# Moving a 128x128 transpose of attention weights from TensorE to a DMA, in a fused decoder layer

## The reference

```python
h = h + 0.5 * swiglu(rms_norm(h, ffn1_norm), ffn1_w_in, ffn1_w_out)     # hidden width 2816
n = rms_norm(h, mix_norm)
gm_u, gm_v, sb_q, sb_k, sb_v = split(n @ w_mix_in)                      # 512 channels each
gm_out = gelu(gm_u) * (tril(w_s) @ rms_norm(gelu(gm_v)) + b_s)          # in chunks of 128 tokens
# stick-breaking attention, 8 heads of 64, for t > s:
#   z[t,s] = q[t].k[s] / 8
#   A[t,s] = sigmoid(z[t,s]) * prod over s<j<t of (1 - sigmoid(z[t,j]))
sb_out = A @ v
h = h + concat(gm_out, sb_out) @ w_mix_out
h = h + 0.5 * swiglu(rms_norm(h, ffn2_norm), ffn2_w_in, ffn2_w_out)
h = h + sigmoid(rms_norm(h, ple_norm) @ ple_w_gate) * (p @ ple_w_proj)
out = rms_norm(h, final_norm)
```

## Time and profile before

| what | value |
|---|---|
| median of 3 runs | 4325.1 us (4325.03 to 4327.18) |
| the profiled execution's own time | 4324.56 us |
| its span, first to last instruction, slowest core (core 3) | 4323.0 us |
| spans of the 8 cores | 4313.9 to 4323.0 us |
| mean granted TensorE clock, core 3 | 0.903 |
| instructions | 66727 |

### The profile page before, as it was taken

How to read it: one execution, slowest core, us unless ns; L and a number is a source line. 1 busy time by engine, 2 the same in 40 slices (tenths; PEclk the granted TensorE clock), 3 DMA queues, 4 the chain that set the end, 5 groups by cost and what they waited for, 6 DMA issues and landing times.

```text
span 4323.0 us, 66727 instructions; the slowest of 8 cores (4313.9 to 4323.0 us)
## 1 busy us (share of the span) xinstructions
PE 3549.6 (82%) x18821; PEld 1641.0 (38%) x18821; DVE 2812.3 (65%) x3660; ACT 1835.6 (42%) x2945; POOL 1082.2 (25%) x654
## 2 busy tenths in 40 slices
PE   6689787979797988979697997988879877777687
PEld 2234332434343433434243443433434333333233
DVE  3244646355655666567776787867878778887743
ACT  2232434143424444444444454554445445444522
POOL 1111222011212222223232332332323333444300
PEclk9889897989898999989898997988989988898789
DMA  8964694524342334323332333322324221111043
GB/s 278 320 206 124 211 319 148 146 82 127 104 140 83 116 92 141 111 81 111 101 112 83 91 113 88 104 83 72 86 76 118 78 62 43 39 44 43 26 120 102
DMA packets 254387, 499.66 MB, mean 116 GB/s; under 512 B 28074, under 2 KB 47058, under 8 KB 254034
## 3 DMA queue, kind: packets, MB, share of 16 engines
q1 hardware_dynamic: 251858, 493.29, 38.0%
q0 software_dynamic: 2176, 2.10, 0.4%
HBM read 436.03 MB, written 61.34 MB: 115 GB/s over the span
## 4 chain that ended last, share of the span: by engine, by line
PE 53%; DVE 18%; issue 12%; ACT 8%; DMA 3%; SPq 3%; POOL 3%; DVEq 1%; ACTq 0%; POOLq 0%
PE bank L169 49%; DVE P L202 8%; PE bank L172 4%; SPq L208 3%; POOL A L191 3%; ACT bank L182 2%; DVE P L185 2%; DVE xnT L199 2%; ACT AT L182 2%; DVE ef_62 L191 1%; DMA fstv_95<-wts 1%; DVE ef_63 L191 1%; ACT L182 1%; ACT rr L182 1%; DVE hT_56 L199 1%
## 5 line engine op out<-in xcount | busy, mean ns | idle before, releaser
L202 DVE TENSOR_TENSOR_SCAN P<-bank,P,cb 128x512 f32<-128x512 f32 (+3 forms) x1152 | 1375.8, 1194 | 509.0 <-ACT bank L182 414.8
L191 POOL TENSOR_TENSOR A<-P 128x1024 bf16<-128x1024 f32 (+3 forms) x576 | 1008.9, 1752 | 2739.4 <-DVE P L202 1578.1
L182 ACT ACTIVATE AT<-bank 128x1024 bf16<-128x1024 bf16 (+3 forms) x576 | 546.6, 949 | 689.2 <-PE bank L172 688.2
L182 ACT ACTIVATE bank<-bank 128x512 f32<-128x512 f32 (+3 forms) x1152 | 579.7, 541 | 204.5 <-PE bank L169 194.2
L172 PE MATMUL bank<-cb,A 128*128 128x128 bf16 x4224 | 363.8, 233 | 206.9 <-POOL A L191 153.9
L172 PEld LDWEIGHTS bank<-cb,A 128*128 128x128 bf16 x4224 | 295.6, 104 | 382.2 <-issue 317.4
L169 PE MATMUL bank<-AT,vc 128*128 128x256 bf16 x2112 | 360.9, 294 | 34.7 <-DVE mix_59 L185 18.5
L185 DVE COPY P<-P 128x2 f32<-128x2 f32 x448 | 269.2, 601 | 15.9 <-DVE P L202 14.5
L169 PEld LDWEIGHTS bank<-AT,vc 128*128 128x128 bf16 x2112 | 200.8, 103 | 203.5 <-issue 109.7
L182 ACT ACTIVATE ef_62<-bank 128x512 f32<-128x512 f32 x240 | 142.9, 595 | 305.9 <-PE bank L169 287.2
L182 ACT ACTIVATE ef_63<-bank 128x512 f32<-128x512 f32 x240 | 142.7, 594 | 228.8 <-PE bank L169 217.4
(11 more groups left out here) (237 smaller groups left out, 4643.4 us busy)
## 6 DMA issues: line engine op xcount, KB each, us to landing
ring_73<-wscr SPq DMA_DIRECT2D x102, 256.0 KB, 2.7
ring_76<-wscr SPq DMA_DIRECT2D x101, 256.0 KB, 2.6
ring_67<-wscr SPq DMA_DIRECT2D x101, 256.0 KB, 2.6
ring_70<-wscr SPq DMA_DIRECT2D x101, 256.0 KB, 2.7
ring_71<-wscr SPq DMA_DIRECT2D x100, 256.0 KB, 2.7
ring_74<-wscr SPq DMA_DIRECT2D x100, 256.0 KB, 2.7
ring_77<-wscr SPq DMA_DIRECT2D x100, 256.0 KB, 2.6
ring_68<-wscr SPq DMA_DIRECT2D x99, 256.0 KB, 2.7
```

Source lines behind the costliest of these rows:

```text
L182: return lambda e: e.activation(out, in_, func, **kw)
L191: return lambda e: e.tensor_tensor(out, in0, in1, op)
L202: return lambda e: e.tensor_tensor_scan(out, d0, d1, initial, op0, op1)
```

## The change

The transposes leave PE and ACT: one DMA per step, issued by SP, transposes the whole 128x1024 `A` buffer into `AT` as eight 128x128 blocks. `A` is zeroed once, since the DMA reads all of it in diagonal steps too. `AT` gets four buffers, and `stage_v` runs five steps after `stage_a` (LAG) where it ran three after. The carry column moves from DVE to POOL, with its own dependency (`Pc`), and the scan takes its start from the buffer of the step before. The copies out of bank 4 move from DVE to ACT and go to a single buffer `sbT`; a new gate `O` holds the first of them until the mix-out projection of the tile before is emitted. Bank 3 goes to the side stream. In ple, the product is written back to PSUM, not to the SBUF buffer `ef`. The costs handed to the scheduler are new, and an engine no longer waits in the model for its own results.

```diff
+SA = 2
+ST = 4
+LAG = 5
-MM_NS = 1.0 / 2.2
+MM_NS = 0.475
...
+def f_dmat(out, in_):
+    return lambda e: e.dma_start_transpose(out=out, in_=in_)
...
-        side = BankPool([5, 6, 7])
-        wide = BankPool([0, 1, 2, 4, 5, 6, 7])
+        side = BankPool([3, 5, 6, 7])
+        wide = BankPool([0, 1, 2, 3, 4, 5, 6, 7])
...
-                S.op("dve", f_tt(efb[i][:, :], efb[i][:, :], B(bj), ALU.mult), reads=[ef_res[i], bank_res[bj]], writes=[ef_res[i]], cost=dve_cost(T))
-                S.op("dve", f_tt(hT[:, j, :], hT[:, j, :], efb[i][:, :], ALU.add), reads=[ef_res[i]] + hr(j), writes=hr(j), cost=dve_cost(T))
+                S.op("dve", f_tt(B(bj), efb[i][:, :], B(bj), ALU.mult), reads=[ef_res[i], bank_res[bj]], writes=[bank_res[bj]], cost=dve_cost(T))
+                S.op("dve", f_tt(hT[:, j, :], hT[:, j, :], B(bj), ALU.add), reads=[bank_res[bj]] + hr(j), writes=hr(j), cost=dve_cost(T))
...
-                if kc == ti:
-                    S.op("dve", f_memset(Pb[:, s, :, c0:c0 + 1], 1.0), writes=[P_res[s]], cost=90.0)
-                else:
-                    S.op("dve", f_copy(Pb[:, s, :, 0:1], Pb[:, 1 - s, :, T:T + 1]), reads=[P_res[1 - s]], writes=[P_res[s]], cost=90.0)
...
-                S.op("pool", f_tt(Ab[:, s, :, c0:T], Pb[:, s, :, c0:T], Pb[:, s, :, c0 + 1:T + 1], ALU.subtract), reads=[P_res[s]], writes=[A_res[s]], cost=2 * n_ * 2.2 + 120)
+                    init = 1.0 if kc == ti else Pb[:, 1 - s, h, T:T + 1]
...
+                if kc == ti:
+                    S.op("pool", f_memset(Pb[:, s, :, c0:c0 + 1], 1.0), writes=[Pc_res[s]], cost=150.0)
+                else:
+                    S.op("pool", f_copy(Pb[:, s, :, 0:1], Pb[:, 1 - s, :, T:T + 1]), reads=[P_res[1 - s]], writes=[Pc_res[s]], cost=150.0)
+                sa = n % SA
+                S.op("pool", f_tt(Ab[:, sa, :, c0:T], Pb[:, s, :, c0:T], Pb[:, s, :, c0 + 1:T + 1], ALU.subtract), reads=[P_res[s], Pc_res[s]], writes=[A_res[sa]], cost=2 * n_ * 1.65 + 205)
...
             def stage_t(n):
-                s = n % 2
-                k0 = c_lo(n) // 128
-                for kb in range(k0, 4):
-                    for h in range(2):
-                        o0 = (kb * 2 + h) * 128
-                        S.op("pe", f_tr(banks[3][:, o0:o0 + 128], Ab[:, s, h, kb * 128:(kb + 1) * 128], identb), reads=[A_res[s], R_const], writes=[bank_res[3]], cost=60.0)
-                act(ATb[:, s, k0:4, :].rearrange("p a b -> p (a b)"), banks[3][:, k0 * 256:1024], AF.Copy, [bank_res[3]], [AT_res[s]])
+                s = n % ST
+                sa = n % SA
+                S.op("sp", f_dmat(ATb[:, s, :, :], Ab[:, sa, :, :].rearrange("p h t -> p (h t)")), reads=[A_res[sa]], writes=[AT_res[s]], dma="t%d" % s, cost=1300.0)
...
-                        S.op("dve", f_copy(mixb[ti % 2][r, 4 + hp, qb * 128:(qb + 1) * 128], B(4)[r, h * 128:(h + 1) * 128]),
-                             reads=[bank_res[4]], writes=[mix_resb[ti % 2][4 + hp]], cost=dve_cost(128))
+                        act(sbT[r, hp, qb * 128:(qb + 1) * 128], B(4)[r, h * 128:(h + 1) * 128], AF.Copy, [bank_res[4]], [sb_res[hp]])
...
-            for n in range(N + 3):
-                if 0 <= n - 2 < N:
-                    yield [A_res[n % 2], bank_res[3]]
-                    stage_t(n - 2)
+            for n in range(N + LAG):
...
+                m = n - LAG
+                if 0 <= m < N:
+                    ti = items[m][0]
+                    if items[m][3] == 0 and ti > 0 and items[m][1:3] == (0, 0):
+                        yield ("gate", ("O", ti - 1))
+                    yield [AT_res[m % ST], bank_res[4]]
+                    stage_v(m)
+                if 0 <= n - 1 < N:
+                    stage_t(n - 1)
```

More of the change, by code:

```diff
@@ L43, in __init__, with ready @@
         self.dma_clk = 0.0
-    def ready(self, reads, writes):
+    def ready(self, reads, writes, eng):
         t = 0.0
         for r in reads:
-            if r.wt > t:
+            if r.we != eng and r.wt > t:
                 t = r.wt
         for w in writes:
-            if w.wt > t:
+            if w.we != eng and w.wt > t:
                 t = w.wt
-            if w.rt > t:
-                t = w.rt
+            for e, v in w.rt.items():
+                if e != eng and v > t:
+                    t = v
         return t + LAT
@@ L63, in op @@
         o.val = 0
-        start = max(self.clk[eng], self.ready(reads, writes))
+        start = max(self.clk[eng], self.ready(reads, writes, eng if dma is None else None))
         if dma is None:
@@ L113, in op @@
                 r.r[key] = o
-            r.rt = max(r.rt, end)
+            r.rt[eng if dma is None else key] = end
         for w in writes:
@@ L118, in op @@
             w.wt = end
-            w.rt = 0.0
+            w.we = eng if dma is None else key
+            w.rt = {}
         self.q[eng].append(o)
@@ L322, in build @@
     xnT, _ = salloc("xnT", [128, 8, T], BF16)
-    mixb = [salloc("mix%d" % i, [128, 8, T], BF16)[0] for i in range(2)]
+    gmb = [salloc("gm%d" % i, [128, 4, T], BF16)[0] for i in range(2)]
+    sbT, _ = salloc("sbT", [128, 4, T], BF16)
     pT, _ = salloc("pT", [128, 2, T], BF16)
@@ L339, in build @@
     print("SBUF used %d of %d" % (off[0], top))
-    banks = [nc.alloc_psum_tensor("bank%d" % i, [128, 1024] if i == 3 else [128, 512], BF16 if i == 3 else F32) for i in range(8)]
+    banks = [nc.alloc_psum_tensor("bank%d" % i, [128, 512], F32) for i in range(8)]
     bank_res = [Res("bank%d" % i) for i in range(8)]
@@ L418, in act @@
         def act(out, in_, func, reads, writes, **kw):
-            S.op("act", f_act(out, in_, func, **kw), reads=reads, writes=writes, cost=fsize(in_) * 0.75 + 180)
+            S.op("act", f_act(out, in_, func, **kw), reads=reads, writes=writes, cost=fsize(in_) * 0.875 + 135)
         def dve_cost(n):
-            return n * 1.05 + 110
+            return n * 1.05 + 145
         S.op("sp", f_dma(cst[:, :], cst_d[:, :]), writes=[R_init], dma="c0")
+        S.op("pool", f_memset(Ab[:, :, :, :].rearrange("p a h t -> p (a h t)"), 0.0), writes=A_res)
         S.op("sp", f_dma(graw[:, :], norms_d[:, :]), writes=[R_init], dma="c1")
@@ L643, in mix_out_gen @@
                 b = bp.next()
-                for y in proj8(w, b, mixT, lambda k: [mres[k]]):
-                    yield y
+                for half, src in ((0, gmb[hb]), (1, sbT)):
+                    yield [w.res] + mres[4 * half:4 * half + 4] + ([bank_res[b]] if half == 0 else [])
+                    for kk in range(4):
+                        k = 4 * half + kk
+                        mm(b, B(b), w.ap[:, k * 128:(k + 1) * 128], src[:, kk, :], k == 0, k == 7, [w.res, mres[k]])
                 if j > 0:
@@ L768, in stage_a @@
                     S.op("pe", f_mm(B(zb[h])[:, c0:T], qTb[ti % 2][r, hp, qb * 128:(qb + 1) * 128], kT[r, hp, kc * T + c0:(kc + 1) * T], True, True),
-                         reads=[q_resb[ti % 2][hp], kT_res[hp][kc]], writes=[bank_res[zb[h]]], cost=n_ * MM_NS / 2 + 30)
+                         reads=[q_resb[ti % 2][hp], kT_res[hp][kc]], writes=[bank_res[zb[h]]], cost=n_ * MM_NS / 2 + 75)
                 for h in range(2):
```

55 lines of the change are left out of this document (27 added, 28 removed).

## The result

The changed kernel takes 3923.5 us (median of 4 runs, 3922.9 to 3926.3) against 4326.1 beside it: ratio 0.907, 95% interval 0.9054 to 0.9086. That is 403 us less; 498 were forecast, and the time lies inside the forecast range. The change's own gain is 4325.0 - 3922.9 = 402 us.

What follows compares the result with a forecast made beforehand. PE was taken to bound stages 1 to 6, the attention loop with DVE fullest stage 7. 4324.6 - 279 - 81 - 111 - 30 + 3 = 3827, about 3830 us; 3760 to 3900 had 50%, 3730 to 4070 about 80%.

Steps and rivals of the forecast that it cites:

- Transposes off PE: Stages 0 to 6: PE's busy time on transposes vanishes and counts whole, since PE is the bound; 279 us saved.
- Waits of PE: Stages 4 to 6: PE's idle time falls to the 61 us of stages 2 and 3; 81 us saved.
- Stage 7: Last stage: 295 us with side work plus 181 us of 58 steps alone, 476 in all; 111 us saved.
- ple and the fourth bank: Adds into hT, ahead of squares PE waits for, shorten from 2.02 to 0.69 us; 30 us saved.
- Carry column: Carry copy moved to POOL costs 0.3 us a step there, hidden; its gain is already in the other terms.
- The DMA: Each transposing DMA lands in 4 us and fills the engines 1.5 us; hidden except for 3 us.
- The first: Rival: PE's stalls reappear at the next norm or bank, only busy time goes; 3960 us, chance 20%.
- The second: Rival: the A buffer binds as transposes land late (7 to 9.3 us); 3925 to 4270 us, chance 12%.
- third: Rival: the DMA engines bind from stage 3 on and the kernel is slower, some 5500 us at 6.7; chance 9%.

Runs made afterwards that it cites:

- e8: Eight TensorE transposes of a constant tile, which wait for nothing and nobody reads, added in each step of the changed kernel, bank 3 given to them: 4031.5 us.
- e9: As e2, with four A buffers, transposes three steps behind the scans instead of two, and output matmuls four behind: 4052.4 us.
- e1: The changed kernel with the planner's numbers and readiness rule as they were before the change: 3929.1 us.
- e2: The changed kernel with the eight TensorE transposes and their ScalarE evacuation back, bank 3 taken from side work, steps as before: 4193.9 us.
- e10: The changed kernel with old planner's numbers and readiness rule, ple through the SBUF tile and carry copies on VectorE: 3990.9 us.
- e5: The changed kernel with three AT buffers instead of four and output matmuls four steps behind instead of five: 3915.9 us.
- e6: As e5, with three A buffers instead of two: 3911.3 us.

## Why the prediction was right, point by point

**Direction, range and most of the size** held: 3830 forecast, 3923.5 measured, in the range of 3730 to 4070, with the DMA as priced. The mechanism of the largest term was mis-sized.

- *Transposes off PE, 279 us.* This is the step that failed: "Up to stage 6, where PE is the bound, I count the busy time whole." e8 puts the same occupation at 115 us with the bank and 85 to 90 without, over all stages, and e9 against the changed kernel agrees: 248 us of transposes in stages 2 to 6 for 134 us of time, bank and evacuation included. TensorE is busy without a gap only in dense stretches (60 of 60 us at the full clock); elsewhere part of the work taken from it comes back, as idle time (79 of the 370 us in e8) or as longer matmuls at a lower granted clock (178).
- *Waits of PE, 81 us.* PE's idle time in stages 4 to 6 came down to 213 us from 264, so 50. The planner's numbers aren't the cause (212 in e1), and neither is the distance to the subtraction: e2, with the transposes on TensorE and the old distance, already has 218, and e9 206. e10, which has the DMA but not the planner's numbers, the ple edit or the carry copies on POOL, has 229. So none of these edits carries it alone. What e2 and e10 share, the split output buffer with its gate and copies on ScalarE, wasn't tried apart, so the cause stays open.
- *Stage 7, 111 us.* It was 137. The end alone runs at 2.83 us a step instead of 3.12, the first part took 278 us (from 3284 to the first scan of the end at 3562) instead of 295. That it is depth and not the DMA (e9: 446 us) wasn't in the prediction.
- *ple and the fourth bank, 30 us.* 56 and 30 when measured one by one. The 1.0 us that an add saves is on the path almost whole; I had counted 30 of 85 us for both edits.
- *Carry column.* 0.19 us on POOL instead of 0.3, but not quite hidden: scans wait 46.3 us in all for POOL, 23.1 of it for this copy. Its move is worth 23 us, which I had left inside other terms.
- *The DMA.* Landing 3.1 us, 1.5 us of the engines, PE waiting 7 us for it: as taken or better. The Trainium skill, "VectorE: DVE Perf Modes", section "The three transpose paths", states 1309 ns for one block by DMA. Eight times that, the estimate of 10.5 us a step, does not agree with this trace, where eight blocks in one instruction land together in 3.1 us; a single block was not run. The Trainium skill, "Advanced Engine Details and Errata", section "X-Bar Transpose (TRN2)", states 350 to 400 GB/s. The estimate from it, 0.7 us a step, is nearer, against 1.5 us of the engines measured.
- *The rivals.* The first (the stalls stay) did not come as told: PE's idle time fell to 656 us, near the 640 of my sum, though the waits for scans grew. What was missing was busy time that came back, which no rival had. The second and third did not come: AT cost PE 7.4 us, more A buffers 0.1%, and the DMA share stood at 0.64.

That the total came within 100 us of the forecast is in part luck: the first two terms together were some 200 us too high, and stage 7, ple with the bank, and the carry copies some 100 too low.

In sum, by gains: the edits around (planner, ple, carry, separate buffers) give 126 us with the transposes still on TensorE, one step of distance with its A buffers 139, and the DMA 137, of which about 90 are TensorE's time and 30 the bank it frees. About 17 of the last and 36 of the first weren't tried apart; candidates are the evacuation on ScalarE and the split output buffer with its gate.

## What to carry to other kernels

Before pricing work taken off the fullest engine, split its busy time by windows: where it has idle places or a lowered clock, expect part of the work to come back and look at the chains of the other engines. Here 370 us of occupation added to an engine that was busy 83% of the time cost about 115. When an in-order engine waits for a late producer, try one more step of distance first: here it gave as much as the move to another engine. Adding the same occupation back without its waits is the experiment that tells the two apart.

## What the runs showed of the hardware

- A transposing DMA of 256 KB (128 x 1024 in bf16) made 1056 packets, (860114 - 251858) / 576, about eight times those of a weight load of that size (493.29 MB in 251858 packets of the kernel before, 2 KB each), yet it landed in 3.1 us and filled the engines for 1.5 us.
- The share of time of the same DMA traffic differs by core: 63.5% in the profile of e5 and 72.8% in that of e6 for equal bytes, with weight loads landing in 3.2 and 4.5 us, at nearly the same kernel time. Within that one execution of e6, six cores stand at 0.64 or 0.65 over the first 3900 us, core 0 at 0.71 and core 1 at 0.74. Why wasn't tried; the 1.5 us has that uncertainty (0.6 us).
- 1632 matmuls added in the thin stretches, 150 us of TensorE's time, did not lengthen the kernel: the granted clock rose from 0.89 to 0.91 and the other matmuls shrank by 120 us.
